# Eight buffers and two chunks side by side for the first norm's columns, with their copies ahead of the first weight blocks' high parts

## What is computed

```
for l in range(2):
    mod  = silu(c)     @ w_mod[l] + b_mod[l]     # 6 x 1024 numbers for the latent tokens
    modc = silu(c_ctx) @ w_mod[l] + b_mod[l]     # the same for the context tokens
    sh1, sc1, g1, sh2, sc2, g2 = split(mod, 6)
    h  = rms_norm(x,  g_norm1[l]) * (1 + sc1)  + sh1
    hc = rms_norm(xc, g_norm1[l]) * (1 + scc1) + shc1
    p, pc = h @ w_in[l], hc @ w_in[l]            # feeds three mixers and three gates
    ...                                          # mLSTM, latent attention, neighbourhood attention
    x = x + g1 * merge(...)
    x = x + g2 * (square(relu(norm2(x) @ w_ff1[l])) @ w_ff2[l])
```

## Time and profile before

| | us |
|---|---|
| median of 3 runs (lowest, highest) | 1616.5 (1615.98, 1617.84) |
| profiled execution, its own time | 1617.22 |
| its span in the trace | 1615.5 |
| PE busy | 1540.5 (95% of the span) |
| DVE / ACT / POOL busy | 1019.9 / 744.6 / 691.8 |
| first matmul of the first product starts at | 46.12 |

### The profile page before, as it was taken

One profiled execution on the slowest core, in us unless ns is written; L12 is line 12 of the kernel. 1 busy time (PEld: TensorE's weight loads), 2 busy tenths in 40 slices (PEclk: granted clock), 3 DMA queues, 4 the chain that ended last, 5 costly groups with the idle time before them and its releaser, 6 DMA issues.

```text
span 1615.5 us, 24884 instructions
## 1 busy us (share of the span) xinstructions
PE 1540.5 (95%) x9666; PEld 1322.1 (82%) x9666; DVE 1019.9 (63%) x1722; ACT 744.6 (46%) x1518; POOL 691.8 (43%) x405
## 2 busy tenths in 40 slices
PE   7899999999999998999999998989998999989998
PEld 3787789877887686788888886988997887989998
DVE  5758936883467764678596957245337387766554
ACT  4425543464545643523223234356436656564442
POOL 0453434724343013455455543565455651234442
PEclk9999999999999999999999999999999999999999
DMA  8453545502144132243454853233421432545553
GB/s 330 183 213 118 179 142 170 186 25 81 61 146 161 31 132 102 75 173 114 182 193 161 298 182 131 72 125 106 141 101 53 153 112 99 183 141 193 183 185 108
DMA packets 69988, 231.17 MB, mean 143 GB/s; under 512 B 18416, under 2 KB 24944, under 8 KB 56560
## 3 DMA queue, kind: packets, MB, share of 16 engines
q1 hardware_dynamic: 60880, 214.19, 37.7%
q10 hardware_dynamic: 8992, 15.39, 2.7%
HBM read 216.98 MB, written 12.58 MB: 142 GB/s over the span
## 4 chain that ended last, share of the span: by engine, by line
PE 74%; DVE 12%; ACT 5%; POOL 4%; issue 4%; DMA 2%; SPq 1%; ACTq 0%; POOLq 0%; DVEq 0%
PE bank L1900 40%; PE bank L1982 9%; PE bank L1938 7%; PE bank L1920 4%; PE bank L1964 3%; PE bank L2293 2%; PE bank L2269 2%; ACT wH L845 2%; PE bank L2280 2%; DVE mjunk L1309 2%; DVE acc L1312 2%; POOL wL L703 1%; PE bank L2143 1%; POOL wL L705 1%; POOL arena L776 1%
## 5 line engine op out<-in xcount | busy, mean ns | idle before, releaser
L845 ACT ACTIVATE wH<-raw 128x768 fp32r<-128x768 f32 (+5 forms) x396 | 298.1, 810 | 395.9 <-PE bank L1900 291.3
L703 POOL TENSOR_TENSOR wL<-raw,wH 128x1280 fp32r<-128x1280 f32 (+2 forms) x143 | 298.1, 2084 | 425.5 <-ACT wH L845 407.1
L705 POOL TENSOR_TENSOR wL<-raw,wH 128x768 fp32r<-128x768 f32 (+3 forms) x198 | 329.6, 1665 | 343.8 <-ACT wH L845 343.7
L1900 PE MATMUL bank<-hH,wH 128*128 128x512 f32 (+1 forms) x720 | 246.8, 343 | 3.2 <-POOL wL L705 1.5
L1900 PE MATMUL bank<-hH,wL 128*128 128x512 f32 (+1 forms) x720 | 244.5, 340 | 0.0
L1900 PE MATMUL bank<-hL,wH 128*128 128x512 f32 (+1 forms) x720 | 244.5, 340 | 0.0
L1900 PE MATMUL bank<-oH,wH 128*128 128x512 f32 (+1 forms) x576 | 193.7, 336 | 0.5 <-issue 0.5
L1900 PE MATMUL bank<-oL,wH 128*128 128x512 f32 (+1 forms) x576 | 193.5, 336 | 0.0
L1900 PE MATMUL bank<-oH,wL 128*128 128x512 f32 (+1 forms) x576 | 193.5, 336 | 0.0
L1312 DVE SCALAR_TENSOR_TENSOR acc<-acc,cb 128x1024 f32<-128x1024 f32 x88 | 165.6, 1895 | 2.5
L1900 PEld LDWEIGHTS bank<-hH,wH 128*128 128x128 f32 x720 | 136.5, 190 | 20.8 <-POOL wL L705 2.1
(11 more groups left out here) (214 smaller groups left out, 3046.7 us busy)
## 6 DMA issues: line engine op xcount, KB each, us to landing
raw<-in_p_ff SPq DMA_DIRECT2D x64, 1024.0 KB, 4.8
acc<-in_p_mod SPq DMA_DIRECT2D x44, 1024.0 KB, 5.7
raw<-in_p_ml SPq DMA_DIRECT2D x12, 1024.0 KB, 5.4
raw<-in_p_na SPq DMA_DIRECT2D x12, 1024.0 KB, 5.4
raw<-in_p_mgc SPq DMA_DIRECT2D x16, 512.0 KB, 3.6
raw<-in_p_mga SPq DMA_DIRECT2D x16, 512.0 KB, 3.6
raw<-in_p_mgb SPq DMA_DIRECT2D x16, 512.0 KB, 3.8
raw<-in_p_out SPq DMA_DIRECT2D x8, 1024.0 KB, 4.9
```

Source lines behind the costliest of these rows:

```text
L703: pool.tensor_tensor(l_[:, 0:cut], r_[:, 0:cut], h_[:, 0:cut].bitcast(F32), ALU.subtract)
L705: pool.tensor_tensor(l_[:, cut:k * w], r_[:, cut:k * w], h_[:, cut:k * w].bitcast(F32), ALU.subtract)\
L845: act.activation(flat(wH, n)[:, part], flat(raw, n)[:, part], ACT.Copy)\
L1900: ins = pe.matmul(dst, w_[:, kk, c:c + P], r_[:, kk, lo:TOK], start=kk == k0 and m == 0, stop=kk == k0 + kn - 1 and m == 2)
```

## The change

`k_raw` gets three more buffers, so that each of the eight chunks has its own; the new three lie where the raw tokens lay, and the sixth load waits until PE has turned these. SP's order of loads changes: all chunks are loaded ahead of mod 3, and the first weight blocks ml 0 and ml 1 behind it. PE takes two chunks at once, into partitions 0-1 and 64-65 of the same banks; ACT copies four half rows instead of two rows, and does this ahead of the high parts of ml 0 and ml 1; PE makes 16 transposes instead of 8, into banks 2 and 3; DVE adds the two halves. DVE makes its cut of ml 0's and ml 1's low parts behind the scaling of chunks 0 and 1 and no longer ahead of the bias.

```diff
         k_raw = [view(at, D) for at in (12288, 13312, 14336, 6144, 7168)]
+        k_raw += [view(at, D) for at in (8192, 9216, 10240)]
...
             def load_columns(i):
-                if i >= len(k_raw):
-                    sp.wait_ge(*S("k_done").at(i - len(k_raw) + 1))
-                sp.dma_start(k_raw[i % len(k_raw)], a["p_modk"][i]).then_inc(S(f"k_full{i % len(k_raw)}").handle, 16)
+                if i == 5:
+                    sp.wait_ge(*S("x_cols").at(KC))
+                sp.dma_start(k_raw[i], a["p_modk"][i]).then_inc(S(f"k_full{i}").handle, 16)
...
             load_columns(0)
             load_mod(1)
-            for i in range(1, 5):
+            for i in range(1, 4):
                 load_columns(i)
             load_mod(2)
+            for i in range(4, KC):
+                load_columns(i)
+            load_mod(3)
             load_all("ml", 0, range(2))
-            load_columns(5)
-            load_mod(3)
-            load_columns(6)
-            load_columns(7)
...
             for c in range(KC):
                 square(0, 0, 0, c)
+            for b in range(2):
+                act.wait_ge(*S(("k_row", "k_done")[b]).at(1))
+                for h in range(2):
+                    r = slice(64 * h, 64 * h + 2)
+                    ins = act.activation(k_row[r, 512 * b:512 * b + 512], bank[b][r, :], ACT.Copy)
+                ins.then_inc(S("k_out").up(1), 1)
             ahead(-1)
-            for b in range(2):
-                act.wait_ge(*(S("k_done").at(KC) if b else S("k_row").at(1)))
-                act.activation(k_row[0:2, 512 * b:512 * b + 512], bank[b][0:2, :], ACT.Copy).then_inc(S("k_out").up(1), 1)
...
                 for c in range(0, KC, 2):
                     scaled(c)
                     scaled(c + 1)
+                    if (l, which, c) == (0, 0, 0):
+                        share_ahead(-1)
...
             for m in range(MOD_START):
                 mod(m)
-            share_ahead(-1)
             dve.wait_ge(*S("par_in").at(S("par_in").n))
             dve.wait_ge(*S("mod_done").at(MOD_START))
             add_bias(0, 0, 8)
-            dve.wait_ge(*S("k_turned").at(1))
-            for s in range(2):
-                link(dve.tensor_tensor(modT[:, 0, 8:16, s], bank[2][:, 0:16].rearrange("p (c s) -> p c s", s=2)[:, :, s],
-                                       par[:, 0, R_BMOD + 8:R_BMOD + 16], ALU.add))
+            dve.wait_ge(*S("k_turned").at(2))
+            for h in range(2):
+                for s in range(2):
+                    link(dve.tensor_tensor(modT[:, 0, 8:16, s], bank[2 + h][:, 0:16].rearrange("p (c s) -> p c s", s=2)[:, :, s],
+                                           modT[:, 0, 8:16, s] if h else par[:, 0, R_BMOD + 8:R_BMOD + 16], ALU.add))
             gains(0, 0)
...
             def columns(i):
-                pe.wait_ge(*S(f"k_full{i % len(k_raw)}").at(16 * (i // len(k_raw) + 1)))
+                for h in range(2):
+                    pe.wait_ge(*S(f"k_full{i + h}").at(16))
                 for b in range(2):
-                    ins = pe.matmul(bank[b][0:2, :], ccol[:, i, :], k_raw[i % len(k_raw)][:, 512 * b:512 * b + 512],
-                                    start=i == 0, stop=i == KC - 1)
+                    for h in range(2):
+                        ins = pe.matmul(bank[b][64 * h:64 * h + 2, :], ccol[:, i + h, :], k_raw[i + h][:, 512 * b:512 * b + 512],
+                                        start=i == 0, stop=i == KC - 2)
...
             columns(0)
-            columns(1)
             columns(2)
             pe.wait_ge(*S("xT_done").at(8))
             for c in range(KC):
                 square_sum(0, 0, 0, c)
-            for i in range(3, KC):
-                columns(i)
+            columns(4)
+            columns(6)
```

More of the change, by code:

```diff
@@ L2012, in columns @@
             def columns(i):
-                pe.wait_ge(*S(f"k_full{i % len(k_raw)}").at(16 * (i // len(k_raw) + 1)))
+                for h in range(2):
+                    pe.wait_ge(*S(f"k_full{i + h}").at(16))
                 for b in range(2):
-                    ins = pe.matmul(bank[b][0:2, :], ccol[:, i, :], k_raw[i % len(k_raw)][:, 512 * b:512 * b + 512],
-                                    start=i == 0, stop=i == KC - 1)
[L2018 to L2021, removed]
+                    for h in range(2):
+                        ins = pe.matmul(bank[b][64 * h:64 * h + 2, :], ccol[:, i + h, :], k_raw[i + h][:, 512 * b:512 * b + 512],
+                                        start=i == 0, stop=i == KC - 2)
+                    if i == KC - 2:
+                        ins.then_inc(S(("k_row", "k_done")[b]).up(1), 1)
             pe.wait_ge(*S("const_in").at(16))
@@ L2049, in _ @@
                     cc = 4 * b + c
-                    ins = pe.transpose(bank[2][:, 2 * cc:2 * cc + 2], k_row[0:2, cc * P:cc * P + P], ident[0:2, 0:2])
-            ins.then_inc(S("k_turned").up(1), 1)
+                    for h in range(2):
+                        r = slice(64 * h, 64 * h + 2)
+                        ins = pe.transpose(bank[2 + h][:, 2 * cc:2 * cc + 2], k_row[r, cc * P:cc * P + P], ident[r, 64 * h:64 * h + 2])
+                        if (b, c) == (1, 3):
+                            ins.then_inc(S("k_turned").up(1), 1)
             for l in range(DEPTH):
```

## The result

The changed kernel takes 1620.28 us in the median of 18 runs (1618.41 to 1622.09), the kernel before 1617.76 in 18 runs beside it. The ratio is 1.0014, with a 95% interval of 1.0008 to 1.0021: the change costs 1.3 to 3.4 us. The forecast was +1.2 (1617.7 against a median of 1616.5 in three runs). The sign was right, and both stay inside the bound of 0.2%; the size was half of what came.

A forecast was written before the change was run, and what follows sets the result against it. PE, busy 95% of the span, bounds the kernel, so only the start-up before chunk 1 counts. First scaling 1.6 sooner, 2.85 of cuts behind it, chunk 1 1.2 later: 1617.7 against a median of 1616.5, range 1614.9 to 1620.9.

The forecast's parts named there:

- Loads: Start-up loads: queue runs dry at 19.7, mod 2 lands as before, mod 3 at 32.8, 1.9 sooner than before.
- PE and ACT: Start-up: last pairs of chunks end at 33.6, copies at 35.6, n_std waits for ml 1's high part until 41.1.
- POOL against the small instructions: Before the first scaling: POOL's rests of 1.85 a block, moved to 37.5 and 39.8, meet DVE's small bias and gain instructions.
- S: Start of DVE's first scaling, 43.52 before; forecast 41.9, between 41.1 and 42.6.
- From S to T: First scaling to PE's chunk 1: 6.82 before, forecast 9.65 with 2.85 of weight cuts in between, POOL starving until DVE pauses.
- T: Time at which PE takes chunk 1 of the first product, 50.34 before; forecast 51.5, 1.2 later.
- the first rival: Behind the weight cuts: POOL gets in ahead of DVE's first hL, PE starts 1.28 late, time 1618.7; chance 0.14.
- Distance kept behind chunk 1: From 52 to the end: both traces keep one distance, everything behind chunk 1 moving rigidly, 1.2 later.
- a sign of being wrong: Prediction wrong if S comes below 40, the pairs stay serial, or the distance grows or shrinks behind chunk 1.
- the four rivals: POOL ahead of hL 1618.7 (0.14), mild gain 1616.0 (0.20), serial pairs 1620.9 (0.09), full gain 1614.6 (0.04).

The follow-up runs named there:

- rest_later: The changed kernel, but POOL does its rests of the low parts of ml 0 and ml 1 behind its hL of chunks 1 and 3; 0.9997 of the kernel before.

## Why the prediction was right or wrong

The stretch in which the prediction expected the load queue to run dry, in the changed kernel (its last number is the rate in GB/s):

```profile
20.00:21.00 1.00, 0.36 (x4) 0.12 (x4) 0.96 (x3) 0.54 (x2) 0.00 (x0) 1.00 0.56 94
```

- **Loads: right.** The queue ran dry: 94 GB/s between 20 and 21 where 414 flowed before. mod 3 was on DVE at 33.09 (32.8 forecast), ml 0 at 35.57 (35.3), ml 1 at 38.03 (37.9). Only mod 2 came 0.6 later than before; that delayed nothing behind it, since mod 3 was what DVE waited for next.
- **PE and ACT: right.** The pairs ended at 33.67 (33.6), the copies at 35.26 (35.6), n_std was there at 41.41 (41.1).
- **POOL against the small instructions: right in kind.** S was 42.17, where 41.9 was taken between ends of 41.1 and 42.6. rest_later shows the cause. The course was another one, though. The prediction priced the second rest alone; in fact the first rest held the first addition for 1.6 us, and so the gains were still to come when the second rest ran. And only the gains came behind it, not five small instructions, since the additions that read a bank went through beside POOL. That 41.9 came so near is in part luck.
- **From S to T: this step failed.** The prediction let POOL starve through the cuts and the first hL as it had through scalings, and put T at S + 9.65. In fact POOL got in behind the second cut, PE started at S + 6.42 instead of S + 5.45, and needed 3.97 for chunk 0 instead of 3.85: T = S + 10.39. That is the first rival, S + 10.6, to which 0.14 was given; its 52.5 is the measured 52.56. PE's 0.12 is the clock, which came back during chunk 0 in the kernel before and only with chunk 1 here. The error was to carry the behaviour of a row (between scalings of 0.4 us) over to another kind of instruction (a cut of 1.44) without bounding it, although the same trace has a row at 53.64 in which POOL was let in at once. The Trainium skill's rule ("SBUF — State Buffer", "Summary: rules for kernel authors"), that of a DVE and a GpSimd instruction the second to issue waits until the first finishes, holds behind the cuts, seven of seven, and at 53.64 in the kernel before, and fails at 46.62; it deserved an even chance.
- **Distance kept behind chunk 1: right up to 326, not for the spans.** It is 2.22 at T and 2.11 at the next product, and then grows by 1.1 with PE's clock; the prediction had named such a growth as a sign of being wrong. That everything behind T moves rigidly with it does not hold in general: over the 14 traces N - T varies by 1.0, nearly as much as the 1.2 that was forecast.
- **The time itself proves little.** The range of 1614.9 to 1620.9 holds 1620.28, but also the times of three of the four rivals, so the rows above bear the account and not the total.

Where did the gain go that the new order seems to bring? mod 3's 1.6 and the cuts' 2.89 were off the way to S. The small instructions with POOL's rests in between gave back 2.9 (4.1 from the end of mod 3 to S, where six such instructions took 1.2 before), and the cuts with POOL's hL stand between S and PE's start, 3.8 more than before. At T 0.25 of that is not seen, since PE had waited for POOL's hL there before.

## What to carry to other kernels

When a load moves, the work of the other engines on it moves too, and here that of POOL moved into the stretch where DVE was waited for; look up what POOL does in every critical DVE stretch before moving weights. Where two waits end within a microsecond, removing one gains at most the distance between them; both have to go. An access that one row shows starving may be let in elsewhere: read every row of its kind in the trace, and price both. And follow a gain past the first matmul that it moves, since up to 1.0 us of it was lost to a later return of PE's clock.

## What was not expected of the hardware

DVE instructions that touch 8 columns in 0.18 us each can be held until a POOL instruction ends: a pair of 0.36 took 1.78. Those that read a bank were not held (0.37 for the pair at 40.33). Whether POOL gets in between two short DVE instructions changes between traces of unchanged code (nine of 14 in layer 1 got in), and costs or gives back 2.4 us of POOL's time. A met wait in front of the DVE instruction had no part in it in two kernels. And PE's clock came back 3.1 to 6.1 us after the first matmul of the same product.
